# Where the squares of two norms are added up: GpSimd in place of VectorE at the ends of the first and last FFN

## The reference, cut to what matters

```python
def rms_norm(x, g):
    xf = x.astype(jnp.float32)
    y = xf * lax.rsqrt(jnp.mean(xf * xf, axis=-1, keepdims=True) + RMS_EPS)
    return (y * g.astype(jnp.float32)).astype(x.dtype)
...
    x = x + 0.5 * swiglu(rms_norm(x, ffn1_norm[l]), ffn1_w1[l], ffn1_w3[l], ffn1_w2[l])
    h = rms_norm(x, mix_norm[l])
    p = h @ w_in[l]
...
    x = x + 0.5 * g3x * swiglu_2(modulate(rmsnorm(x, norm_ffn2[l]), sh3x, sc3x), w13_ffn2[l], w2_ffn2[l])
    return rmsnorm(x, norm_final)
```

## Time and profile before

| what | us |
|---|---|
| median of 3 runs | 1649.91 (1647.41 to 1651.48) |
| the profiled execution, its own time | 1648.0 |
| its span | 1646.2 |
| PE busy | 1627.7 (99% of the span) |
| DVE busy | 1115.4 (68%) |
| ACT busy | 698.3 (42%) |
| POOL busy | 23.9 (1%) |

### The profile page before, as it was taken

One profiled execution on the slowest core, in us unless ns is written; L12 is line 12 of the kernel. 1 busy time (PEld: TensorE's weight loads), 2 busy tenths in 40 slices (PEclk: granted clock), 3 DMA queues, 4 the chain that ended last, 5 costly groups with the idle time before them and its releaser, 6 DMA issues.

```text
span 1646.2 us, 30278 instructions
## 1 busy us (share of the span) xinstructions
PE 1627.7 (99%) x12552; PEld 1477.9 (90%) x12552; DVE 1115.4 (68%) x1617; ACT 698.3 (42%) x918; POOL 23.9 (1%) x41
## 2 busy tenths in 40 slices
PE   9999999999999999999999999999999999999998
PEld 7999888899999999988888887988999999999997
DVE  7666657564887766668887874967457676676665
ACT  6444456434455444421222122516354445454443
POOL 1000000000000000000000000000000000000000
PEclk9999999999999999999999999999999999999998
DMA  7555477322265545243456542233323355545551
GB/s 292 178 188 194 154 283 265 120 79 105 104 237 180 203 178 195 98 158 140 164 193 253 193 166 77 103 128 104 108 77 112 146 183 187 194 154 189 192 180 52
DMA packets 37837, 267.80 MB, mean 163 GB/s; under 512 B 4268, under 2 KB 4524, under 8 KB 5744
## 3 DMA queue, kind: packets, MB, share of 16 engines
q1 hardware_dynamic: 33552, 238.25, 40.5%
q0 software_dynamic: 4192, 28.19, 4.5%
HBM read 265.38 MB, written 1.05 MB: 162 GB/s over the span
## 4 chain that ended last, share of the span: by engine, by line
PE 73%; issue 23%; DVE 3%; ACT 1%; DMA 0%; POOL 0%; POOLq 0%; SPq 0%; DVEq 0%; ACTq 0%
PE PS L436 15%; PE PS L437 15%; PE PS L442 11%; PE PS L655 9%; PE PS L828 6%; PE PS L659 5%; PE PS L684 2%; PE PS L892 1%; DVE W_LO L430 1%; PE PS L540 1%; PE PS L872 1%; PE PS L874 1%; PE PS L873 1%; PE PS L1178 0%; PE PS L1353 0%
## 5 line engine op out<-in xcount | busy, mean ns | idle before, releaser
L430 DVE TENSOR_TENSOR W_LO<-RAW,W_HI 128x2048 fp32r<-128x2048 f32 x210 | 476.2, 2269 | 181.8 <-ACT W_HI L418 180.9
L418 ACT ACTIVATE W_HI<-RAW 128x2048 fp32r<-128x2048 f32 x208 | 397.6, 1913 | 362.1 <-PE PS L442 239.9
L436 PE MATMUL PS<-HS,W_HI 128*128 128x256 f32 (+1 forms) x792 | 265.3, 339 | 1.5 <-ACT G L1732 0.8
L437 PE MATMUL PS<-HS,W_LO 128*128 128x256 f32 (+1 forms) x792 | 261.5, 334 | 0.0
L655 PE MATMUL PS<-HS,W_HI 128*128 128x512 f32 x984 | 246.5, 392 | 0.7 <-DVE W_LO L430 0.7
L442 PE MATMUL PS<-HS,W_HI 128*128 128x512 f32 (+1 forms) x712 | 242.1, 340 | 0.0
L436 PE MATMUL PS<-HID_HI,W_HI 128*128 128x256 f32 (+1 forms) x720 | 220.6, 307 | 0.3 <-DVE XC L2598 0.3
L437 PE MATMUL PS<-HID_HI,W_LO 128*128 128x256 f32 (+1 forms) x720 | 220.2, 307 | 0.0
L655 PEld LDWEIGHTS PS<-HS,W_HI 128*128 128x128 f32 x984 | 177.0, 189 | 32.6 <-DVE W_LO L430 0.9
L436 PEld LDWEIGHTS PS<-HS,W_HI 128*128 128x128 f32 x792 | 150.1, 189 | 19.7 <-issue 3.3
L437 PEld LDWEIGHTS PS<-HS,W_LO 128*128 128x128 f32 x792 | 150.2, 190 | 14.9
(11 more groups left out here) (442 smaller groups left out, 2425.6 us busy)
## 6 DMA issues: line engine op xcount, KB each, us to landing
RAW<-stream SPq DMA_DIRECT2D x225, 1024.0 KB, 4.8
LATE<-stream POOLq DMA_DIRECT2D x24, 1024.0 KB, 5.1
XC<-xin SPq DMA_DIRECT2D x2, 512.0 KB, 4.6
XC<-xin POOLq DMA_DIRECT2D x1, 1024.0 KB, 5.1
out<-NT SPq DMA_DIRECT2D x4, 256.0 KB, 2.6
CON<-consts POOLq DMA_DIRECT2D x1, 616.0 KB, 6.5
LW<-lora POOLq DMA_DIRECT2D x1, 512.0 KB, 6.7
DFT<-dft POOLq DMA_DIRECT2D x1, 266.0 KB, 2.9
```

Source lines behind the costliest of these rows:

```text
L418: nc.scalar.activation(W_HI[s % RING][:], RAW[PLACE[u]][:], ACT.Copy).then_inc(hi_done, 1)
L430: last = nc.vector.tensor_tensor(W_LO[s % RING][:, o], RAW[PLACE[u]][:, o], W_HI[s % RING][:, o].bitcast(F32), ALU.subtract)
L436: nc.tensor.matmul(acc, w_hi, x_hi, start=first, stop=False)
L437: return nc.tensor.matmul(acc, w_lo, x_hi, start=False, stop=last)
```

## The change

The additions of squares at the end of `ffn1` and `ffn4` go from VectorE's program to GpSimd's, with the same waits on `norm_sq` and `norm_acc`. For `nb` they stand behind the four table loads and ahead of the load of `XC[:, 1]`; for `nj` behind the load of `EDGE` and ahead of the two last multiplications. On ScalarE the two scaled copies go behind `root("nj")`. All other norms stay as they were.

```diff
+            def pool_squares(name):
+
+                for k in range(1, NORM_ADDS[name] + 1):
+                    pool.wait_ge(S("norm_sq"), KT * NORM[name] + k + 1)
+                    if k > 1:
+                        pool.wait_ge(S("norm_acc"), NORM_ACC[name] + k - 1)
+                    nc.gpsimd.tensor_tensor(NT[:, 0], NT[:, 0], NT[:, k], ALU.add).then_inc(S("norm_acc"), 1)
+
...
             pool.dma_start(MOD[:], bada).then_inc(S("tables_in"), 16)
+            pool_squares("nb")
             pool.wait_ge(S("gate_sig"), 1)
...
             pool.dma_start(EDGE[:], edge).then_inc(S("dft_in"), 16)
+            pool_squares("nj")
             pool.wait_ge(S("row_scale"), 4)
...
                 square("nj", 0, k, "down_added", DOWN_BASE[3] + k + 1 + (k == KT - 1))
+            root("nj")
             for k in range(6, KT):
                 A(SG2[:, k - 6], XC[:, 0, k], ACT.Identity, scale=par("mf", k)).then_inc(S("row_scale"), 1)
-            root("nj")
...
                         into(m, BK8[4 + m // 2][:, m % 2 * ROWS:(m % 2 + 1) * ROWS])
-                        if then != "nd" and 2 <= m <= NORM_ADDS[then] + 1:
-                            add_squares(then, m - 1)
```

## The result

The changed kernel takes 1654.13 us (median of 15 runs, 1651.51 to 1655.42) against 1650.06 us before (15 runs, 1647.41 to 1651.89). The ratio is 1.0023 with a 95% interval of 1.0015 to 1.0030: slower by 0.23%, about 4 us, where 0.17% had been forecast. (A ratio here is taken over all runs and needn't be the quotient of the two medians.) The profiled execution took 1653.63 us, its span is 1651.8 us.

A forecast was written before the change was run, and what follows sets the result against it. TensorE, busy 99% of the span, was taken to bound the kernel. To the median of 1649.9 us came 1.7 us at the end of ffn1 and 1.1 us at the program's end: 1652.7 us, range 1649.0 to 1656.5.

The forecast's parts named there:

- The path: Both places: GpSimd's chained additions decide; the last square comes 1.5 us (ffn1) and 1.4 us (end of program) earlier, unawaited.
- GpSimd's step: Both places: each chained addition on GpSimd takes 0.81 us, made of 0.72 us operation and 0.09 us wait.
- The collision: End of ffn1: VectorE's half split, held up by GpSimd's third addition, goes ahead of the fourth, 201.9 to 203.1.
- Sums to scaling: End of ffn1: TensorE's sums start at 204.73 and end at 206.28; ada work and spreading follow, scaling at 207.96.
- The term of 1.7 us for this place: End of ffn1: the first scaling starts at 207.96 in place of 206.22, 1.7 us later.
- the second rival: End of ffn1: TensorE's clock falls in the longer wait, costing 1.6 to 4.6 us; 1655.7 us, chance 0.17.
- the forecast: Whole kernel: both places get later, VectorE's half split goes between GpSimd's additions; 1652.7 us, chance 0.53.
- The formula of 16p - 4p - 1.2: End of program: delay with p us per weight load; +0.4 us at clock 1.00, +1.6 us at 0.50.
- The 1.1 us taken: End of program: 1.1 us later, with the clock falling in the middle of the new sums.
- The scaled copies: End of program, ScalarE: old and new places are both covered by waits, so moving them changes 0.
- steps of 0.70 us: Both places: the shortest step taken for GpSimd's additions; about 0 at ffn1 without collision, -0.3 at the end of the program.
- the best ends of both places: Whole kernel: the most favourable outcome at ffn1 and at the program's end, lower limit of the range, 1649.0 us.

The follow-up runs named there:

- run 3: The changed kernel with VectorE waiting for all five additions of squares of nb before its first half split; 1653.08 us, ratio 1.0021.
- run 4: The changed kernel with five matmuls (results unused) on TensorE between the last down product of ffn1 and the sums of nb; 1652.28 us, ratio 1.0018.
- run 2: The kernel before with only the additions of nj on GpSimd and the scaled copies behind the root; 1651.35 us, ratio 1.0007.
- run 8: The kernel before with only the scaled copies behind the root; 1648.63 us, ratio 0.9995.
- run 7: The kernel before with unused matmuls in TensorE's waits, two behind ffn1 and one behind ffn4; 1647.96 us, ratio 0.9992.
- run 1: The kernel before with only the additions of nb on GpSimd, scaled copies ahead of the root; 1653.22 us, ratio 1.0018.
- the first four experiments: run 1, run 2, run 3 and run 4, which shared 33 runs of the kernel before; those took 1650.01 us.
- run 6: The kernel before with three additions on VectorE in each place and sums in the order 4, 5, 6, 0, 7; 1647.98 us, ratio 0.9986.

## Why the prediction was right

**The path.** That both places hang on the additions and no longer on the last square, and that VectorE's freed time buys nothing, came out as written: TensorE waits for GpSimd at both, and the last square is 1.5 us (from 2.84 to 1.33 us behind the last down matmul's start, 203.88 and 202.70) and 1.4 us earlier, for nobody.

**GpSimd's step.** An addition takes 0.72 to 0.74 us, as rows 5 have it for that size. The step is 0.88 us and not 0.81: the wait for its own result costs 0.14 us, where I took the 0.09 us of its wait for ScalarE. Over the steps of a place that is some 0.3 us. At the end of ffn1 that was given back by luck: the fourth addition ended 0.59 us behind the split, where I had 0.8.

**The collision.** It came where it was put, in favour of VectorE: its half split, up during the third addition, lost 0.05 us at most and went ahead of the fourth. Sums 3.57 us behind the last down matmul; forecast 3.69 (201.04 to 204.73). Run 3 shows it by taking it away. The Trainium skill (SBUF — State Buffer, "SBUF: two separate sides") has whichever engine starts first hold the port pair to the end of its instruction; run 3 and the changed kernel agree, with 0.72 against 1.52 us for the same addition.

**Sums to scaling.** 3.2 us was forecast from the start of the sums to the first scaling, and run 4 has 3.18 us (204.73 to 207.91) at full clock. The term of 1.7 us for this place is 6.75 - 5.18 = 1.6 us at full clock.

**The clock.** This is the step that was set too low. I gave its fall a chance of 0.17, with rows of before that show none. By the sign that I had named, the clock between 201 and 210 us, the profile of the changed kernel shows the second rival and not the forecast, and the measured 1654.13 us lies midway between the forecast's 1652.7 and the rival's 1655.7. But run 2 and run 8 have a fall at the same place with the additions on VectorE, so the rival had the wrong thing to compare with: before pays for a fall as well. What a fall costs can be read from the last down matmul of ffn1 to an operation behind the dense work, VectorE's reciprocal of SQK. That operation in before, run 2, run 4 and the changed kernel, where the last down matmul starts at 201.04, 201.03, 201.16 and 201.37:

```profile
241.51 1.75 DVE L2294 RECIPROCAL SQK<-SQK 128x256 f32<-128x256 f32 x1 [0.64 <-ACT SQK L1652]
242.91 1.75 DVE L2303 RECIPROCAL SQK<-SQK 128x256 f32<-128x256 f32 x1 [0.64 <-ACT SQK L1661]
243.20 1.75 DVE L2304 RECIPROCAL SQK<-SQK 128x256 f32<-128x256 f32 x1 [0.64 <-ACT SQK L1664]
246.41 1.75 DVE L2302 RECIPROCAL SQK<-SQK 128x256 f32<-128x256 f32 x1 [0.64 <-ACT SQK L1662]
```

| last down matmul of ffn1 to this reciprocal, us | no fall at ffn1 | fall at ffn1 | the fall costs |
|---|---|---|---|
| chain of before | 40.47 (before), 40.46 (run 7) | 41.88 (run 2), 41.90 (run 8) | 1.4 |
| chain of the change | 42.04 (run 4) | 45.04 (changed), 45.03 (run 1) | 3.0 |
| difference | 1.6 | 3.15 | |

The 3.0 us are the middle of the 1.6 to 4.6 that the prediction had as the fall's price; of them before pays 1.4 in executions with a fall. In the changed kernel the fall comes ahead of the sums, so sums, ada work and spreading all run at half speed; in run 2 it comes in the spreading, in run 8 in the ada work.

A second fall, between 430 and 450 us, where the change does nothing (PEclk 0.83 from 435 to 445, 1.00 before), is in the profile of the changed kernel and not in that of before. It costs 0.7 us by two other reciprocals of VectorE on either side of it: they start at 432.41 and 479.19 in before, at 437.54 and 485.06 in the changed kernel. The profile of before was a lucky one: its mean clock was 0.997, as only 5 of the 33 runs beside the first four experiments have it, and these average 0.9953. Each run lists its mean clock, and the times sort by it:

| mean granted clock | before, us (runs) | changed, us (runs) |
|---|---|---|
| 0.994 | 1651.38 (10) | 1654.46 (6) |
| 0.995 | 1649.99 (8) | 1653.92 (6) |
| 0.996 | 1649.60 (10) | 1652.56 (1) |
| 0.997 | 1648.16 (5) | 1651.51 (1) |

At equal mean clock the changed kernel is 3.0 to 3.9 us slower, two of the four lines resting on a single run. Its own average is 0.9947, which by the slope of the table (3.2 us for 0.003) goes with another 0.6 us. That isn't a comparison at full clock: both may spend the same time at half speed in different places.

**The end of the program.** The formula of 16p - 4p - 1.2 gave 0.4 us at full clock and 1.6 at half. At full clock the first scaling starts 0.3 us later (5.27 us behind the last down matmul in the changed kernel and run 4, 4.95 in run 7), and GpSimd's last multiplication ends 0.4 us later (7.74 and 7.34): the formula's 0.4. Two small misses cancel in it: TensorE starts the sums 2.02 us behind the last down matmul where I had 1.85, and sixteen records take 1.95 us where I had 2.2. D2 differs by 11.71 - 11.03 = 0.7 us; the other 0.3 us lie behind that multiplication, in the writing out (3.97 and 3.69 us), and no run shows why. At half clock D2 is 12.91 (run 2) and 13.42 (run 3) against 11.95 and 11.99: 0.9 to 1.5 us. The 1.1 us taken was in the middle.

**The scaled copies.** Zero, as said (run 8).

**The sum.** 1652.7 forecast, 1654.13 measured; 2.8 us more than before forecast, 4.07 measured. At full clock the two places make 1.6 + 0.7 = 2.3 us. With a fall on both sides they make 3.15 us, which is the 3.2 us that run 1 lost, and 0.9 to 1.5 us: 4.1 to 4.6, the size of what the medians show. So the term that was too small is the one of the end of ffn1, 1.7 us, which holds at full clock alone. That these profiles stand for the usual execution of each kernel is argued and not shown: it would need the clock of every run place by place. Two bounds of the prediction don't follow from its terms: with steps of 0.70 us the formula gives 0 at the end of the program and not -0.3, and the best ends of both places give 1649.9 us or, with the -0.3, 1649.6, not 1649.0. The forecast doesn't rest on them.

## What to carry to other kernels

When a serial chain feeds an engine that works in order, count what stands behind the last arrival and not who makes it: moving the additions to an engine with the longer step (0.88 us against 0.67) made the chain longer, while summing the tiles in the order in which they come, with fewer additions, took 3.3 us off with the additions on GpSimd and 2.4 us with them on VectorE, part of it through the clock. An operation put on GpSimd has to be checked against every VectorE operation with two SBUF inputs in its time. A chain that ends later also costs more when the clock falls in it: 3.0 us here where the shorter one pays 1.4. And if one profile of a kernel has the clock at 1.00 in a short wait, look at the mean clock of its other runs before taking that as the rule.

## What the runs showed of the hardware

The falls of the clock come and go between executions of one program, and in these kernels they have their places: in stretches of 10 us, all twelve profiles taken here (before, changed and the ten runs) have the clock at 1.00 outside 200 to 220 us, 430 to 450 us and what follows 1630 us. Eight of the twelve have a fall at the first place (not before, runs 4, 6 and 7) and nine at the second (not before, runs 6 and 7), with the same instructions there. In the chain of before the first costs 1.4 us, the second 0.7 us, and one at the end of the program 0.9 us (D2 of 11.95 against 11.03): 3.0 us together, where the runs of before with a mean clock of 0.994 and 0.997 lie 3.2 us apart. A wait of GpSimd for its own result costs 0.14 us beyond the 0.73 us of the operation.
